# Overflow loop of an expert layer moved ahead of the last expert pair; last gathers made plain, their sums made on VectorE

## The chip, the cores and the metric

One core of one Trainium2 chip runs the program. The metric is the device time of one execution in microseconds. Before the change it is 790.01 us, the median of 3 runs (789.26 to 790.51).

## What is computed

One layer of a streaming encoder block on 512 tokens of width 1024, in float32: an input projection, a windowed attention and a state-space branch mixed by gates, a LayerNorm (h1), then the part that matters here:

```
g      = argmax of the 4 group logits of a token; its weight is the softmax value
e1, e2 = the two best of the 8 experts in that group, weights by softmax times the group's
moe    = sum over e1, e2 of weight * (silu(h1 @ w_gate[e]) * (h1 @ w_up[e])) @ w_down[e]
ple    = sigmoid(h1 @ w_ple_gate + b) * (p @ w_ple)
out    = LayerNorm(2**0.25 * h1 + moe + ple; ln2_w, ln2_b)
```

There are 32 experts, with matrices of 1024 x 256 (gate, up) and 256 x 1024 (down). Every token goes to two of them.

## The kernel before

**The expert stage.** Each expert gets 64 rows (`CAP`). Experts are worked off in 16 pairs of 128 rows; pair `p` has parity `p % 2`, and each parity has six weight slots of 1 MB in `ring` (parity 0: slots 0 to 5, parity 1: slots 6 to 11). SyncE loads a pair's weights as soon as the pair two before it has used its slots. GpSimd fetches the rows of a pair from `h1_dram` by an indirect DMA. TensorE turns them (`rows_turned_in`), multiplies them with gate and up (`gate_up`, L1256), ScalarE makes the tanh (`hidden_tanh`), VectorE the product (`hidden`, L2184 to L2189), TensorE turns that (`act_t`, L1281), ScalarE copies it (`act_copy`), TensorE multiplies with down (`down`, L1271). ScalarE and VectorE copy one half each of the result out of PSUM (`out_copy`, `out_half`), and GpSimd stores the 128 rows to `y_dram`, at places given by `storeU` (L844). Between these stand the pieces of `ple` (`ple_half`, `ple_sum`, `ple_out`), which add to `base`, the array that starts as 2**0.25 * h1 and in the end is the output.

**The last pair.** The result of pair 15 (`LAST`) is not stored. VectorE writes a matrix `last_rows` with each token's weight at the row where its result lies (`rows_weighted`, L2194 to L2202), TensorE turns it (`rows_turned`, L1287) and ScalarE copies it back (`last_rowsT`). In the kernel before this stands inside pair 14: TensorE turns it between `act_t` and `down` of pair 14. At the end TensorE multiplies `last_rowsT` with the pair's result, once for each of the 4 tiles of 128 tokens (`combine`, L1294), and VectorE adds the product to `base` (`added`, L2208).

**The overflow loop.** Rows beyond 64 of an expert would be worked off in a loop of up to 8 turns (`MORE_PAIRS`), whose body is entered only if the count in `ctl` asks for it. Each engine reads the count and goes through the 8 turns. With these inputs no turn is entered: the trace holds loads for exactly 32 experts. In the kernel before the loop stands after `gate_up` and `hidden` of the last pair and before its `act_t`.

**The gathers.** When the store of pair 14 has landed, GpSimd fetches for each tile the two result rows of each token from `y_dram` (L854), with a DMA that adds to `base`: the first results of tiles 0 to 3, then the second, each of which waits until the first of its tile has landed (`y_gath[i]`). `added` of a tile waits for both.

**The end.** ScalarE makes the LayerNorm sums of tiles 0 and 1 (`tile_stats`, L1382 to L1386: a sum pass and a square pass over 1024 elements), VectorE those of tiles 2 and 3 (L1676). TensorE spreads the rows ln2_w and ln2_b over the partitions by products with a one-row operand (L1360). Then VectorE makes the roots (L1681 and on) and normalizes tiles 0 to 2 in six passes (L1685, L1686); ScalarE and GpSimd do tile 3; ScalarE issues the four output DMAs.

The order of work of each engine is written out by hand; an engine goes through its queue in that order and waits where a `wait_ge` stands.

## Time and profile before

| | us |
|---|---|
| median of 3 runs | 790.01 (789.26 to 790.51) |
| profiled execution, its own time | 789.76 |
| its span, first to last instruction | 787.0 |
| TensorE busy | 728.7 (93%) |
| VectorE / ScalarE / GpSimd busy | 418.4 / 204.1 / 184.0 |
| DMA, mean rate over the span | 220 GB/s |

Busy times are sums over the span; the page's slices of 19.7 us show TensorE at 90% or more almost everywhere until the last few. In the eleven slices from 512 to 728 us, where the expert weights stream in, the DMA engines are at 90% or more, at 410 to 421 GB/s. What the change touches lies in the last 62 us. The difference between the execution's time and its span, 2.8 us, lies outside the instructions. The granted clock of TensorE has two levels here, shown as 1.00 (2.4 GHz) and 0.50 (1.2 GHz).

### The profile page before, as it was taken

The numbers are of one execution on the slowest core, as the hardware profiler recorded it, in microseconds if no ns is written. First come the engines' busy times: TensorE is split into PE (matmuls) and PEld (weight loads), VectorE is DVE, ScalarE is ACT, GpSimd is POOL, SyncE is SP. The second block draws the span as 40 slices with busy tenths as digits, with TensorE's granted clock in tenths as the row PEclk, the third lists the DMA queues.
The fourth block names the chain that finished last, engine by engine and source line by source line (L and its number), as shares of the span: only waits on it lengthen the run. The fifth ranks groups of instructions, "written<-read, shape, count | busy, mean of one in ns | idle before, by whom it ended". The sixth has DMA issues, their size and how long they took to land.

```text
span 787.0 us, 9738 instructions
## 1 busy us (share of the span) xinstructions
PE 728.7 (93%) x3799; PEld 512.9 (65%) x3799; DVE 418.4 (53%) x737; ACT 204.1 (26%) x358; POOL 184.0 (23%) x129
## 2 busy tenths in 40 slices
PE   4999999999999999999999999999999989897672
PEld 2897789998887878847888888445544444343220
DVE  6598946776678888655266957412121112121226
ACT  4313324555322223242041151111211121111030
POOL 4934490000041222002242003311111111111242
PEclk9999999999999999999999999999999999999985
DMA  9798131321031122243233298699999999999492
GB/s 309 268 410 201 58 108 54 94 69 54 4 105 54 54 54 54 65 176 110 104 143 152 102 399 329 215 419 415 415 410 417 421 419 419 421 420 416 154 201 107
DMA packets 61816, 173.15 MB, mean 220 GB/s; under 512 B 16982, under 2 KB 39712, under 8 KB 47946
## 3 DMA queue, kind: packets, MB, share of 16 engines
q1 hardware_dynamic: 52324, 141.79, 47.9%
q0 software_dynamic: 8752, 28.59, 11.1%
q10 hardware_dynamic: 694, 2.14, 0.7%
q8 instruction: 31, 0.51, 0.3%
q14 instruction: 15, 0.12, 0.0%
HBM read 155.52 MB, written 24.67 MB: 229 GB/s over the span
## 4 chain that ended last, share of the span: by engine, by line
PE 76%; DMA 12%; DVE 6%; issue 2%; POOL 1%; ACT 1%; SPq 0%; DVEq 0%; POOLq 0%
PE psum L902 37%; PE psum L1256 11%; DMA ring<-in_w_exp_up_dram 6%; PE psum L1271 5%; PE psum L1174 5%; PE psum L1111 3%; DMA ring<-in_w_in_dram 3%; PE psum L1060 2%; PE psum L1080 1%; PE psum L1212 1%; PE psum L1010 1%; DMA arena<-y_rows,rowsU 1%; PE psum L1177 1%; DMA arena<-in_w_ple_gate_dram 1%; PE psum L979 1%
## 5 line engine op out<-in xcount | busy, mean ns | idle before, releaser
L902 PE MATMUL psum<-ring_r 128*128 128x512 f32 (+1 forms) x928 | 247.5, 350 | 3.3 <-DVE arena_r L1695 1.7
L902 PEld LDWEIGHTS psum<-ring_r 128*128 128x128 f32 x928 | 164.1, 192 | 28.3 <-issue 3.2
L902 PE MATMUL psum<-arena_r,ring_r 128*128 128x512 f32 (+1 forms) x416 | 141.4, 377 | 0.0
L751 POOL TENSOR_TENSOR ring_r<-ring,ring_r 128x2048 fp32r<-128x2048 f32 x16 | 73.9, 4621 | 204.5 <-ACT ring_r L1369 204.5
L1256 PE MATMUL psum<-ring,arena 128*64 128x512 f32 x512 | 112.9, 593 | 5.3 <-DMA ring<-in_w_exp_up_dram 5.3
L1369 ACT COPY arena<-psum 128x512 f32<-128x512 f32 (+4 forms) x104 | 57.4, 580 | 172.3 <-PE psum L1271 55.8
L1256 PEld LDWEIGHTS psum<-ring,arena 128*64 128x64 f32 x512 | 39.5, 137 | 76.0 <-issue 76.0
L902 PEld LDWEIGHTS psum<-arena_r,ring_r 128*128 128x128 f32 x416 | 79.6, 191 | 13.7 <-issue 0.5
L1271 PE MATMUL psum<-ring,arena 128*64 128x512 f32 x256 | 61.1, 620 | 9.0 <-issue 9.0
L1174 PE MATMUL psum<-arena 128*128 128x256 f32 x256 | 64.5, 398 | 2.3 <-DVE rowsU L2153 1.2
L2184 DVE SCALAR_TENSOR_TENSOR arena<-arena,psum 128x256 f32<-128x256 f32 x16 | 9.7, 609 | 104.0 <-ACT arena L1584 103.9
L1174 PEld LDWEIGHTS psum<-arena 128*128 128x128 f32 x256 | 48.0, 197 | 20.3 <-issue 14.6
L1369 ACT CAST ring_r<-ring 128x2048 fp32r<-128x2048 f32 (+1 forms) x26 | 45.8, 1768 | 23.4 <-DMA ring<-in_w_in_dram 13.2
L1271 PEld LDWEIGHTS psum<-ring,arena 128*64 128x64 f32 x256 | 19.2, 142 | 41.4 <-issue 41.4
L2215 DVE COPY arena<-psum 128x512 f32<-128x512 f32 x16 | 11.1, 692 | 60.2 <-PE psum L1271 60.2
L902 PE MATMUL psum<-ring_r,arena_r 128*128 128x256 f32 (+1 forms) x144 | 41.4, 295 | 0.0
L810 POOL DMA_INDIRECT arena<-h_rows,info x14 | 14.3, 1021 | 115.6 <-PE psum L1212 106.9
L844 POOL DMA_INDIRECT y_rows<-arena,storeU x15 | 15.0, 1003 | 83.7 <-DVE arena L2215 83.0
L1584 ACT ACTIVATE arena<-psum 128x256 f32<-128x256 f32 x16 | 6.1, 384 | 106.2 <-PE psum L1256 106.2
L1496 ACT ACTIVATE ring<-psum,arena 128x512 f32<-128x512 f32 x16 | 11.0, 688 | 65.0 <-PE psum L902 65.0
L1111 PE MATMUL psum<-arena,ring 128*128 128x512 f32 x64 | 27.6, 592 | 0.0
L902 PEld LDWEIGHTS psum<-ring_r,arena_r 128*128 128x128 f32 (+1 forms) x144 | 26.0, 181 | 2.1
(299 smaller groups left out, 974.8 us busy)
## 6 DMA issues: line engine op xcount, KB each, us to landing
ring<-in_w_exp_up_dram SPq DMA_DIRECT2D x32, 1024.0 KB, 15.3
ring<-in_w_exp_down_dram SPq DMA_DIRECT2D x32, 1024.0 KB, 13.9
ring<-in_w_exp_gate_dram SPq DMA_DIRECT2D x32, 1024.0 KB, 11.2
ring<-in_w_in_dram SPq DMA_DIRECT2D x18, 1024.0 KB, 5.4
y_rows<-arena POOLq DMA_DIRECT2D x12, 1024.0 KB, 17.0
ring<-in_w_out_ssd_dram SPq DMA_DIRECT2D x4, 1024.0 KB, 6.5
ring<-in_w_out_dram SPq DMA_DIRECT2D x4, 1024.0 KB, 5.1
arena<-in_w_ple_gate_dram SPq DMA_DIRECT2D x4, 1024.0 KB, 12.8
```

Source lines behind the costliest of these rows:

```text
L751: g.tensor_tensor(lo, ring[:, SLOT_OF[seq]], hi.bitcast(F32), ALU.subtract).then_inc(s_w_lo, 1)
L810: g.indirect_dma_start(out=xg.rearrange("p k n -> p (k n)"), out_offset=None, in_=h1_dram, in_offset=bass.IndirectOffsetOnAxis(ap=tokens, ...
L844: g.indirect_dma_start(out=y_dram, out_offset=bass.IndirectOffsetOnAxis(ap=storeU[:, p:p + 1], axis=0), in_=eout[:, p % 2, :], in_offset=N ...
L902: t = mm(o, a, b, start=(first and j == 0), stop=(last and j == 2))
L1060: t = mm(o[:, m * P:(m + 1) * P], dta[:, c, hh:hh + 1].broadcast_to([P, P]), upper, start=True, stop=True)
L1111: t = mm(o, ringN[:, s, j % 2, n * P:(n + 1) * P], yaT[:, j, :], start=(j == 0), stop=(j == 3))
L1174: mm(ple_bank(n)[:, 0:PS], h1T[:, i, k, :], pgw[s][:, k, :], start=(k == 0), stop=(k == KD - 1))
L1256: t = mm(psum[sides[half], parity, :], xgT[parity][:, k, sides[half]], ring[:, s:s + 2, k, :], start=(k == 0), stop=(k == KD - 1))
L1271: t = mm(psum[sides[half], 4 + b, :], eactT[:, parity, k, sides[half]], ringN[:, s, k, b * 512:(b + 1) * 512], start=(k == 0), stop=(k == 1))
L1369: return nc.scalar.copy(dst, src)
L1496: A(gact[:, n, b, :], bank(("g", g)), ACT.Tanh, scale=0.5, bias=b_gate[:, 8 * b + n:8 * b + n + 1]).then_inc(s_g_read, 1)
L2215: v.tensor_copy(eout[:, u % 2, 512:1024], psum[:, 5, :]).then_inc(signal, 1)
```

## The change

- **Place of the loop.** On every engine the overflow loop now stands after pair 14 and before `gate_up` of pair 15. On TensorE each turn gets two transposes outside of the guarded body (the `nop` goes), and one more transpose after the loop signals `s_last_aT`.
- **Place of `last_rows`.** VectorE makes it after its copy of pair 14's result, TensorE turns it after `gate_up` of pair 15.
- **Rows of ln2.** The four one-row products stand before and after `act_t` and after `down` of pair 15, no longer at the end.
- **Gathers.** They no longer add: the first results go to slots 0 to 3 of `ring` (`first_res`, `second_res`), so they wait for TensorE to be past the loop (`s_last_aT >= 1`) and no longer for `base`. VectorE adds them (`result_in`): the four first ones before the copy of the last down product, each second one after that copy, before its tile's product is added.
- **Sum.** The add of a tile's product also makes the tile's sum (`added_last`, `tensor_tensor_reduce`); ScalarE makes the squares of all four tiles without a sum pass (`squares_about_mean`). VectorE's `tile_stats` at the end goes.
- `s_base_ready` goes; its waits on VectorE become waits of the common chain. `combine` and `added` take their banks as arguments.

```diff
 MOE_FREED = [("pe_ys", KD) if slot in (4, 5, 6, 7) else ("pe_mix", 2 * NT) for slot in range(12)]
+MORE_BANKS = ((6, 7), (4, 5))
+LAST_BANKS = ((1, 3), (4, 5))
...
...
@@ -846,15 +850,16 @@
                     in_offset=None, bounds_check=ROWS - 1, oob_is_err=False).then_inc(y_st[p % 2], 16)
             for parity in range(2):
                 pool.wait_ge(y_st[parity], 16 * (PAIRS // 2 - parity))
-            pool.wait_ge(s_base_ready, 4 * NT)
-            for c in range(2):
+            pool.wait_ge(s_last_aT, 1)
+            for c, to in enumerate((first_res, second_res)):
                 for i in range(NT):
                     if c:
                         pool.wait_ge(y_gath[i], 16)
                     g.indirect_dma_start(
-                        out=base[:, i, :], out_offset=None, in_=y_dram,
+                        out=to[:, i, :], out_offset=None, in_=y_dram,
                         in_offset=bass.IndirectOffsetOnAxis(ap=rowsU[:, 2 * i + c:2 * i + c + 1], axis=0),
-                        bounds_check=ROWS - 1, oob_is_err=True, compute_op=ALU.add).then_inc(y_gath[i], 16)
+                        bounds_check=ROWS - 1, oob_is_err=True).then_inc(y_gath[i], 16)
...
-                    break
+                rows_turned_in(p + 1)
                 if p == 0:
                     freed(3, 4, 5)
                 act_t(p, p % 2, p, s_aT_mm)
                 for n, half in after_act:
                     ple_half(n, half)
-                if p == LAST - 1:
-                    pe.wait_ge(s_last_rows, 1)
-                    rows_turned(last_rows, s_last_rows)
                 down(p, q, p % 2, (s_aT_sb, p + 1), s_y_mm)
                 for n, half in after_down:
                     ple_half(n, half)
-            pe.wait_ge(s_last_rows, 3)
             pe.wait_ge(s_ctl_ready, 1)
+            pe.wait_ge(s_pp_read, 4 * NT)
             pairs = pe.value_load(ctl[0:1, EXTRA + 1:EXTRA + 2], min_val=0, max_val=MORE_PAIRS)
             with pe.Fori(0, MORE_PAIRS) as j:
...
+                tr(psum[:, 6, 0:P], ident, ident)
+                tr(psum[:, 6, P:2 * P], ident, ident)
+
+            tr(psum[:, 6, 0:P], ident, ident).then_inc(s_last_aT, 1)
+            gate_up(LAST // 2, LAST % 2, 2 * PAIRS, s_last_aT)
+            pe.wait_ge(s_last_rows, 1)
+            rows_turned(last_rows, s_last_rows)
+            pe.wait_ge(s_ln_in, 64)
+
+            def ln2_row(row, b, to):
+
+                return mm(psum[:, to, :], ones[0:1, :], row[0:1, 512 * b:512 * b + 512], start=True, stop=True)
+
+            ln2_row(w_ln2, 0, W_BANKS[0])
+            ln2_row(w_ln2, 1, W_BANKS[1])
             act_t(LAST, LAST % 2, LAST, s_last_aT)
-            down(LAST, LAST // 2, LAST % 2, (s_last_aT, 2), s_last_y)
+            ln2_row(b_ln2, 1, B_BANKS[1])
+            down(LAST, LAST // 2, LAST % 2, (s_last_aT, 7), s_last_y)
+            pe.wait_ge(s_last_rows, 3)
+            ln2_row(b_ln2, 0, B_BANKS[0]).then_inc(s_pe_ln2, 1)
             pe.wait_ge(s_last_y, 3)
             for i in range(NT):
                 if i >= 2:
                     pe.wait_ge(s_last_added, i - 1)
-                combine(last_rowsT, LAST % 2, i, s_last_mm)
-            pe.wait_ge(s_ln_in, 64)
-            for j, row in enumerate((w_ln2, b_ln2)):
-                for b in range(2):
-                    t = mm(psum[:, 2 * j + b, :], ones[0:1, :], row[0:1, 512 * b:512 * b + 512], start=True, stop=True)
-            t.then_inc(s_pe_ln2, 1)
+                combine(last_rowsT, LAST % 2, i, LAST_BANKS[i % 2], s_last_mm)
...
                 act.wait_ge(s_act_sums, sums_made[0])
+
+            def squares_about_mean(x, i, scratch):
+
+                total, minus_mean, squares = (sums[:, i, j:j + 1] for j in range(3))
+                A(mva[:, i, 0:1], total, ACT.Copy, scale=1.0 / D)
+                summed(A(minus_mean, total, ACT.Copy, scale=-1.0 / D))
+                summed(A(scratch, x, ACT.Square, bias=minus_mean, accum_out=squares))
+                A(mva[:, i, 1:2], squares, ACT.Copy, scale=1.0 / D).then_inc(s_act_stats, 1)
...
                     out_copy((s_y_mm, j + LAST + 1), 16 * (PAIRS // 2), 0, s_y_act)
                 act.nop()
-            act_copy((s_last_aT, 1), LAST % 2, s_last_aT)
+            hidden_tanh((s_last_aT, 2), LAST % 2, s_last_aT)
+            rows_turned(last_rowsT, (s_last_rows, 2), s_last_rows)
+            act_copy((s_last_aT, 6), LAST % 2, s_last_aT)
             out_copy((s_last_y, 1), 16 * (LAST // 2), LAST % 2, s_last_y)
-            for i in range(2):
+            for i in range(NT):
                 act.wait_ge(s_last_added, i + 1)
-                tile_stats(base[:, i, :], i, h1_words[:, i, :])
+                squares_about_mean(base[:, i, :], i, h1_words[:, i, :])
             scaled(base[:, NT - 1, :], 1)
...
+                v.tensor_tensor(x, x, from_pe, ALU.add).then_inc(signal, 1)
+
+            def added_last(i):
+
+                dve.wait_ge(s_last_mm, i + 1)
+                banks = LAST_BANKS[i % 2]
+                from_pe = psum[:, banks[0]:banks[1] + 1:banks[1] - banks[0], :]
+                x = base[:, i, :].rearrange("p (b n) -> p b n", b=2)
+                v.tensor_tensor_reduce(out=x, in0=x, in1=from_pe, scale=1.0, scalar=0.0, op0=ALU.add, op1=ALU.add,
+                                       accum_out=sums[:, i, 0:1]).then_inc(s_last_added, 1)
+
+            def result_in(to, i, n):
+
+                dve.wait_ge(y_gath[i], 16 * n)
+                link(v.tensor_tensor(base[:, i, :], base[:, i, :], to[:, i, :], ALU.add))
             def out_half(made, stores, u, signal):
...
-                if p == LAST:
-                    break
                 for n in ple_done(p, 0, 1):
                     ple_sum(n)
                     ple_out(n)
-                if p == LAST - 1:
-                    dve.wait_ge(s_pe_pl, 4 * NT)
-                    rows_weighted(last_rows, -2 * CAP * LAST, 0, s_last_rows)
-                    dve.wait_ge(s_last_rows, 1)
-                    v.tensor_scalar(rowf, rowf, -float(2 * CAP * PAIRS), None, ALU.add).then_inc(s_weighted, 1)
-                    v.tensor_copy(rv[11], rv[8]).then_inc(s_more_added, 1)
                 out_half((s_y_mm, p + 1), 16 * q, p % 2, s_y_dve)
                 for n in ple_done(p, 2):
                     ple_sum(n)
                     ple_out(n)
+
+            dve.wait_ge(s_pe_pl, 4 * NT)
+            rows_weighted(last_rows, -2 * CAP * LAST, 0, s_last_rows)
+            dve.wait_ge(s_last_rows, 1)
+            v.tensor_scalar(rowf, rowf, -float(2 * CAP * PAIRS), None, ALU.add).then_inc(s_weighted, 1)
+            v.tensor_copy(rv[11], rv[8]).then_inc(s_more_added, 1)
...
+                result_in(first_res, i, 1)
             out_half((s_last_y, 1), 16 * (LAST // 2), LAST % 2, s_last_y)
             for i in range(NT):
-                dve.wait_ge(y_gath[i], 32)
-                added(i, (s_last_mm, i + 1), s_last_added)
-                if i >= 2:
-                    dve.wait_ge(s_last_added, i + 1)
-                    tile_stats(base[:, i, :], i)
-            dve.wait_ge(s_act_stats, 2 + 2)
+                result_in(second_res, i, 2)
+                added_last(i)
+            dve.wait_ge(s_act_stats, 2 + NT)
             dve.wait_ge(s_pe_ln2, 1)
-            w2, b2 = (psum[:, 2 * j:2 * j + 2, :].rearrange("p b n -> p (b n)") for j in range(2))
-            tiles_normed(base, w2, b2, s_fin_ready)
+            w2, b2 = (psum[:, banks[0]:banks[1] + 1:banks[1] - banks[0], :] for banks in (W_BANKS, B_BANKS))
+            tiles_normed(base.rearrange("p i (b n) -> p i b n", b=2), w2, b2, s_fin_ready)
 # ---- launch: one core; inputs and outputs as the reference has them ----
```

How the order moves. TensorE, from `act_t` of pair 14 on, before (L1287 turns `last_rows`, L1271 is `down` of pair 14, L1256 `gate_up` of pair 15, L1323 the load of the count ahead of the loop):

```order
L1281 MATMUL psum<-arena 128x128 [waits aT_sb,eact_sb]
L1281 MATMUL psum<-arena 128x128
L1287 MATMUL psum<-arena 128x128 [waits last_rows]
L1287 MATMUL psum<-arena 128x128 x3
L1271 MATMUL psum<-ring,arena 64x512 [waits y_act,aT_sb,y_dve,slot_in5,slot_in2]
L1271 MATMUL psum<-ring,arena 64x512 x7
L1256 MATMUL psum<-ring,arena 64x512 [waits slot_in10,slot_in9,xgT_sb,slot_in7,slot_in6]
L1256 MATMUL psum<-ring,arena 64x512 x15
L1323 TENSOR_LOAD ctl [waits ctl_ready,last_rows]
L1323 ISA x2
```

Now, the same place up to the load of the count:

```order
L1289 MATMUL psum<-arena 128x128 [waits aT_sb,eact_sb]
L1289 MATMUL psum<-arena 128x128
L1276 MATMUL psum<-ring,arena 64x512 [waits y_act,aT_sb,y_dve,slot_in5,slot_in2]
L1276 MATMUL psum<-ring,arena 64x512 x7
L1324 TENSOR_LOAD ctl [waits pp_read,ctl_ready]
```

and from the end of a turn of the loop (L1349, L1350 are its two transposes) through `gate_up` of pair 15 (L1261), the turning of `last_rows` (L1295) and the first row of ln2_w (L1360):

```order
L1349 MATMUL psum<-arena 128x128
L1350 MATMUL psum<-arena 128x128
L1325 REGISTER_ALU
L1325 COMPARE_AND_BRANCH
L1352 MATMUL psum<-arena 128x128
L1261 MATMUL psum<-ring,arena 64x512 [waits slot_in10,slot_in9,xgT_sb,slot_in7,slot_in6]
L1261 MATMUL psum<-ring,arena 64x512 x15
L1295 MATMUL psum<-arena 128x128 [waits last_rows]
L1295 MATMUL psum<-arena 128x128 x3
L1360 MATMUL psum<-arena 128x512 [waits ln_in]
```

`down` of pair 14 no longer has the turning of `last_rows` ahead of it; `gate_up` of pair 15 now has the whole loop ahead of it.

VectorE, from its copy of the last down product on, before:

```order
L2215 COPY arena<-psum 128x512 [waits y_st1,last_y]
L2208 TENSOR_TENSOR arena<-arena,psum 128x1024 [waits last_mm,y_gath0]
L2208 TENSOR_TENSOR arena<-arena,psum 128x1024 [waits last_mm,y_gath1]
L2208 TENSOR_TENSOR arena<-arena,psum 128x1024 [waits last_mm,y_gath2]
L1676 BN_STATS arena<-arena 128x6 [waits last_added]
L1676 BN_STATS arena<-arena 128x6 [waits dve_step]
L1677 BN_AGGR arena<-arena 128x2 [waits dve_step]
L2208 TENSOR_TENSOR arena<-arena,psum 128x1024 [waits last_mm,y_gath3,dve_step]
L1676 BN_STATS arena<-arena 128x6 [waits last_added]
L1676 BN_STATS arena<-arena 128x6 [waits dve_step]
L1677 BN_AGGR arena<-arena 128x2 [waits dve_step]
```

Now, from the last pair's hidden product on (L2199 and L2201; L2248 adds gathered rows, L2254 is the copy, L2242 the add with the sum and the read of its accumulator):

```order
L2199 SCALAR_TENSOR_TENSOR arena<-arena,psum 128x128x2 [waits last_aT]
L2201 TENSOR_TENSOR arena<-arena,psum 128x128x2 [waits last_aT]
L2248 TENSOR_TENSOR arena<-arena,ring 128x1024 [waits y_gath0]
L2248 TENSOR_TENSOR arena<-arena,ring 128x1024 [waits y_gath1,dve_step]
L2248 TENSOR_TENSOR arena<-arena,ring 128x1024 [waits y_gath2,dve_step]
L2248 TENSOR_TENSOR arena<-arena,ring 128x1024 [waits y_gath3,dve_step]
L2254 COPY arena<-psum 128x512 [waits y_st1,last_y,dve_step]
L2248 TENSOR_TENSOR arena<-arena,ring 128x1024 [waits y_gath0]
L2242 ISA arena<-arena,psum 128x1024 [waits last_mm,dve_step]
L2242 ISA arena 128x1
L2248 TENSOR_TENSOR arena<-arena,ring 128x1024 [waits y_gath1]
L2242 ISA arena<-arena,psum 128x1024 [waits last_mm,dve_step]
```

Four adds now stand ahead of the copy, and between two tiles' products there is one add of gathered rows, where the statistics of tiles 2 and 3 were.

## Rows read from the trace of the kernel before

**Rows 1.** Chain of waits at the end: start us, us, what.

```profile
728.95 2.20 DVE arena L2198 x8
...
731.92 1.09 PE psum L1287 x4
...
739.39 3.27 DMA y_rows<-arena,storeU
...
751.02 9.49 DMA arena<-y_rows,rowsU
...
767.21 4.82 PE psum L1360 x8
```

**Rows 2.** Timeline, 706 to 738 us: start us, us, engine, line, operation [idle before].

```profile
709.61 3.65 PE L1271 MATMUL psum<-ring,arena 128*64 128x512 f32 x16 [0.94 <-issue]
...
727.61 0.37 ACT L1369 COPY arena<-psum 128x256 f32<-128x256 f32 x1
...
737.85 0.69 DVE L2215 COPY arena<-psum 128x512 f32<-128x512 f32 x1 [5.70 <-PE psum L1271]
```

**Rows 3.** Timeline, 735 to 788 us.

```profile
737.63 7.03 PE L1256 MATMUL psum<-ring,arena 128*64 128x512 f32 x32
...
745.76 0.60 DVE L2189 TENSOR_TENSOR arena<-arena,psum 128x256 f32<-128x256 f32 x1
...
747.64 0.41 PE L1281 MATMUL psum<-arena 128*128 128x128 f32 x2 [2.98 <-issue]
...
749.60 5.05 PE L1271 MATMUL psum<-ring,arena 128*64 128x512 f32 x16 [1.55 <-issue]
...
760.54 1.22 DVE L2208 TENSOR_TENSOR arena<-arena,psum 128x1024 f32<-128x1024 f32 x1 [5.16 <-DMA arena<-y_rows,rowsU]
...
762.98 0.20 ACT L1383 ACTIVATE arena<-arena 128x1 f32<-128x1 f32 x1
...
764.58 0.20 ACT L1386 ACTIVATE arena<-arena 128x1 f32<-128x1 f32 x1
...
772.17 0.17 DVE L1681 TENSOR_SCALAR arena<-arena 128x4 f32<-128x4 f32 x1 [0.78 <-PE psum L1360]
...
781.02 1.28 DVE L1686 SCALAR_TENSOR_TENSOR arena<-arena,psum 128x1024 f32<-128x1024 f32 x1
```

**Rows 4.** Source view, PE's queue, L1323: ns min/median/max, first and last start us.

```profile
L1323 PEldq TENSOR_LOAD <-ctl x1: 489/489/489, 740.3 to 740.3; - x1
```

**Rows 5.** Source view, PE's loop (L1324): moves and end of turn.

```profile
L1324 PEldq MOVE  x9: 29/29/35, 741.2 to 746.8; - x9
...
L1324 PEldq COMPARE_BRANCH  x8: 86/224/240, 742.0 to 747.4; - x8
```

**Rows 6.** Source view, PE's queue at the waits of down and gate_up.

```profile
L1266 PEldq EVENT_SEMAPHORE  x2: 51/51/51, 732.0 to 749.5; - x2
```

**Rows 7.** Source view, the same at the next gate_up (L611).

```profile
L611 PEldq EVENT_SEMAPHORE  x1: 51/51/51, 733.5 to 733.5; - x1
```

**Rows 8.** Lines by form, DVE: busy us, mean ns.

```profile
L1937 DVE CUSTOM_DVE_ANT_0 arena<-arena 128x512 f32<-128x512 f32 x8 | 5.5, 692 | 0.3
...
L1898 DVE TENSOR_TENSOR arena<-arena 128x1024 f32<-128x1024 f32 x4 | 4.9, 1224 | 0.1
...
L1937 DVE DVE_READ_ACCUMULATOR2_ANT arena<- 128x1 f32 x8 | 0.7, 82 | 0.0
```

**Rows 9.** Lines by form, POOL.

```profile
L810 POOL DMA_INDIRECT arena<-h_rows,info x14 | 14.3, 1021 | 115.6 <-PE psum L1212 106.9 <-DMA info<-row_info 8.7
L854 POOL DMA_INDIRECT arena<-y_rows,rowsU x8 | 12.6, 1576 | 7.3 <-DMA arena<-y_rows,rowsU 3.1 <-DMA y_rows<-arena,storeU 3.0 <-issue 1.2
```

**Rows 10.** Source view of the gathers (L854), with their landing times.

```profile
L854 POOL DMA_INDIRECT arena<-y_rows,rowsU x8: 1559/1562/1661, 743.4 to 758.8; - x8
...
DMA to landing us min/median/max: 8.2/9.0/9.2
```

**Rows 11.** DMA issues around 726.6 us: us to landing.

```profile
arena<-in_ln_b_dram POOLq DMA_DIRECT2D x1, 512.0 KB, 10.9
```

**Rows 12.** DMA issues around 707.1 us.

```profile
ring<-in_w_exp_up_dram SPq DMA_DIRECT2D x1, 1024.0 KB, 26.5
```

**Rows 13.** Windows, PE alone: us, PE busy, granted clock, DMA share, GB/s.

```profile
745.60:749.04 3.44, 0.41 (x2) 1.00 0.98 155
749.05:752.45 3.40, 2.85 (x8) 0.50 1.05 184
752.50:762.69 10.19, 6.72 (x20) 1.00 1.06 209
```

78 lines of the change are left out of this document (39 added, 39 removed).

## The prediction

> **What bounds the kernel now.** I read the chain of waits first, backward from its end, then the timeline of the last 80 us, then the queue instructions, which the timeline leaves out. The reader is to see three stretches.
>
> *Ahead of `down` of pair 14.* ScalarE's copy of the turned activations ends at 727.98 [rows 2], so `down` could start at about 728.1. It starts at 733.01: VectorE first builds `last_rows` (L2198 from 728.95, 2.20 us) and TensorE turns it (731.92, 1.09 us) [rows 1]. It then runs until 737.82, and VectorE's copy starts at 737.85 [rows 2].
>
> *The gathers.* The store of pair 14 starts at 739.39 and takes 3.27 us [rows 1]. The eight gathers start between 743.4 and 758.8, about one per 2.2 us, each landing 8.2 to 9.2 us after its start [rows 10]. Tile 0's second one lands at 760.5 [rows 1]; VectorE sat idle 5.16 us before its first add at 760.54 [rows 3]. `down` of pair 15 had ended at 754.65 (749.60 and 5.05 us [rows 3]). So here the gathers bound the end, not the experts.
>
> *The end.* Adds, statistics and the one-row products (4.82 us, L1360 [rows 1]) run until the roots begin at 772.17; from there to the end of the last normalizing pass at 782.30 and of the span at 787.0 is 14.83 us [rows 3]. No step of that piece changes but for addresses; I count it at nothing.
>
> **The queue of TensorE** is the fourth thing to see. Its count is loaded at 740.3 [rows 4], and the eight turns run from 741.2 to about 747.6 (last branch 747.4) [rows 5], while the array still works on `gate_up` until 744.66 [rows 3]. The loop was thus mostly hidden; only 1.28 us show, since the hidden product was done at 746.36 and `act_t` began at 747.64 [rows 3]. The queue can run ahead: it went from the wait of `down` (732.0) to that of the next `gate_up` (733.5) in 1.5 us [rows 6, 7], while the array needed until 737.8.
>
> **Part by part.**
>
> *`last_rows` out of the way of `down` of pair 14.* `down` starts at 728.2. The same product for pair 13 took 3.65 us [rows 2], here it took 4.81 because it met the half clock. I take 3.65: it ends at 731.85, 5.97 us earlier. VectorE's copy (0.69) ends at 732.6, and `last_rows` follows: 2.20, 1.09 and small ones, done near 736, long before TensorE asks for it. It then costs nothing; without that cover it would cost the 3.2 us it took before.
>
> *The loop ahead of `gate_up` of pair 15.* The queue has issued `down` at 728.1 + 1.5 = 729.6. The load and the first turn begin 0.9 us apart (740.3, 741.2), so turns start at 730.7. A turn took 6.3/8 = 0.79 us [rows 5]. Now it issues two transposes, four records; the 32 records of `down` took 1.5 us to issue [rows 6, 7], 0.047 each, so 0.19 more: 0.98 a turn, 7.8 us, to 738.5. The transpose behind it and the waits of `gate_up` add 0.4: `gate_up` starts at **738.9**, 1.3 us later than the 737.63 of before, though the array is free from 731.85 on. Its weights are there: the last ones were issued at 707.0 and landed 26.5 us later, at 733.5 [rows 12]. So almost all of the 6 us are eaten by the loop. Bounds for a turn: 0.79 (transposes free, 1.5 us less in all) and 1.7 (each record of a transpose as dear as a branch, 0.224 [rows 5]; 5.8 us more). I take the rate at which `down` was issued, the nearest row.
>
> *`gate_up` to `down` of pair 15.* `gate_up` 7.03 us [rows 3], to 745.9. Behind it on TensorE now stand four transposes (0.44 at full clock) and two products of ln2_w. `gate_up` had 16 pairs of records in 7.03 us, 0.44 per pair; a full product is two records one after the other, so two products 1.7 us. They end at 748.1. The hidden product takes 1.70 us after `gate_up` (744.66 to 746.36 [rows 3]), to 747.6: `act_t` is now late by 0.5 because of the products ahead of it. It ends at 748.45, ScalarE's copy (0.37 [rows 2]) at 748.9, the product of ln2_b behind `act_t` ends at 749.3: `down` starts at **749.3**, 0.3 earlier than before. VectorE and ScalarE had done their loops by then.
>
> *The clock.* Before, `down` of pair 15 ran 3.4 us at 0.50 [rows 13], which cost it 5.05 - 3.65 = 1.4 us. In the new order the array is again lightly used ahead of it (transposes, one-row products), so I keep 5.05: `down` ends at 754.35, the copies at 755.1. Bounds: 1.4 less, or one more stretch at 0.50 in `gate_up`, 1.7 more (3.4 us do half the work).
>
> *Gathers.* The store is issued at 732.6 + 0.85 = 733.45, while weights and ln2_b still come in (the latter lands at 726.75 + 10.9 = 737.7 [rows 11], ahead of it in the same queue). I put its landing at 739.5. TensorE's signal comes at 738.6, so the first gather starts at 740.3, 3.1 us earlier. Plain row fetches take GpSimd 1.02 us, adding ones 1.58 [rows 9]. No unloaded plain fetch is in the trace; the nearest are the store (3.27) and the adding gathers (up to 9.2). I take about 4: the first results land from 744 to 749, the second ones until 754. VectorE's four first adds (1.224 each for two operands in SBUF [rows 8], 5.0 in all) start at 747.6 and are done at 752.6, hidden by `down`.
>
> *The adds at the end.* VectorE adds tile 0's second result by 756.3. TensorE makes the last ln2_b product (0.86) and tile 0's `combine` (1.7) from 754.35: 757.0. Each add with a sum: 512 elements took 692 ns, as a plain one of that size, plus an accumulator read of 82 [rows 8]; for 1024 I take 1.22 + 0.08 + gaps = 1.34, then the next tile's gathered add 1.25. Four tiles: 757.05 + 3 x 2.6 + 1.34 = 766.2. `combine` of tiles 1 to 3 (1.7, at half clock 3.4) keeps ahead. ScalarE's rest for the last tile took 762.98 to 764.78, 1.8 us [rows 3]: 768.05. The roots begin at **768.1** in place of 772.17: **4.1 us** earlier. The one-row products and VectorE's statistics are off the path.
>
> **Sum.** 789.76 - 4.1 = 785.7 for the profiled execution, which stands 0.25 below the median; in terms of the median 785.9. I say **785.8**. The 6 us that `down` of pair 14 gains are nearly all taken by the loop, so the last product is only 0.3 us earlier; the gain comes from the gathers, which no longer hold the first add (757.05 for 760.54). From that add to the roots it is 11.0 us, where it was 11.6. What is late next is VectorE.
>
> **Rivals.**
>
> 1. *The clock falls in the loop.* For: before, `act_t`'s two transposes were all that ran from 745.60 to 749.04 and the next 3.4 us were at 0.50 [rows 13]. Against: now 16 transposes run, some 0.22 of each 0.98 us. If `gate_up` meets 3.4 us of 0.50, the end is 1.7 later: 787.5; if `down` then meets none, 786.1. I say 787. The Trainium skill, TensorE: Matmul & The Clock Gate (Part 4, PE-mode transpose), holds that transposes do not count as array work for the clock; by it the loop's transposes are vain and this rival is the likelier. The trace agrees as far as the two transposes go, but it cannot tell them from idleness.
>
> 2. *The gathers still bound.* If plain ones move no faster than the adding ones, landings come 2.45 us apart from 749.3 on; the last of eight is in at 766.5, and 2.6 + 1.8 us later the roots begin at 770.9: 788.6. Against: adding ones read and write the same bytes, and the weight stream moved twice their 209 GB/s [rows 13] (410 to 421 by the page's slices).
>
> 3. *Slower: the loop's turns are dearer.* Place: TensorE's queue, with an empty array behind it. Each turn ends in a taken branch into code that now begins with array instructions. At the upper bound of 1.7 us a turn the loop ends at 744.3, `gate_up` starts 5.8 later than I forecast: 791.6. It decides from 1.5 us a turn on (4.1 us more, no gain). Against: all branches but the first took 0.22 with the queue full.
>
> 4. *Cheaper than forecast*: turns of 0.79 and no half clock ahead of `down`: 1.5 + 1.4 less, 782.9; with only one of the two 784.4.
>
> **Chances.** Forecast 0.47, rival 1 0.22, rival 2 0.08, rival 3 0.09, rival 4 0.14. A measurement can tell about 0.2% (1.6 us) from no change. Rival 3 gives slower 0.07, the rest no change; rival 2 is half no change; a bad end of rival 1 (half clock also in `combine`, 1.7 more) gives the rest of no change. Faster 0.82, same 0.11, slower 0.07. The range runs from 783.3 (part of rival 4) to 788.8 (all of rivals 1 and 2).
>
> **What would show it.** Right: `down` of pair 14 starts at about 728.2 and takes 3.7; the count is loaded near 729.8 and `gate_up` of pair 15 starts within 738 to 740 with nothing to wait for but its own queue; `down` of pair 15 starts near 749; VectorE never waits for a gather behind its last copy; its eight last adds are back to back but for the first; the roots begin near 768. Wrong: `gate_up` at 742 or later (rival 3); a clock of 0.50 under `gate_up` (rival 1); VectorE waiting for `y_rows` (rival 2); an add with a sum that takes over 1.5 us; or a change ahead of 726 us, which no step here foresees.

## The result, and the profile after

The changed kernel takes **784.05 us** (median of 7 runs, 783.24 to 786.09), beside 790.01 us for the kernel before (7 runs on the same chip, 787.93 to 790.96): ratio 0.9931, 95% interval 0.9915 to 0.9946. It is faster by 5.4 us by that ratio (4.3 to 6.7). The forecast was 785.8, with 783.3 to 788.8 as its range. Run again on another chip (`changed_again` below), the kernel gave 0.9918 (0.9894 to 0.9942).

| | before | after |
|---|---|---|
| median, us | 790.01 | 784.05 |
| profiled execution, its own time | 789.76 | 785.12 |
| its span | 787.0 | 783.4 |
| TensorE busy | 728.7 | 727.8 |
| VectorE busy | 418.4 | 425.3 |

The two profiled executions show 3.6 us of span, less than the medians do. One reason is upstream: in the profile of after, ScalarE's copy ahead of `down` of pair 14 ends at 728.88, 0.9 us later than before (727.98 [rows 2]), though nothing ahead of it was changed. So I count from that copy's end, called the anchor here. From it to the roots before took 772.17 - 727.98 = 44.19 us [rows 2, 3]; after it takes 768.51 - 728.88 = **39.63 us**, 4.6 less. From the roots to the end of the span it is 14.9 us, as before (14.8).

The chain of waits of the changed kernel ends like this (start us, us, what):

```profile
729.09 3.67 PE psum L1276 x16
734.38 7.66 DMA y_rows<-arena,storeU
746.83 6.13 DMA ring<-y_rows,rowsU
755.07 5.41 PE psum L1301 x8
```

The building of `last_rows` and the one-row products of [rows 1] are gone from it. The store and a gather are still in it, and the store's piece has grown from 3.27 to 7.66 us.

The timeline of the changed kernel, 728 to 747 us (L1276 is `down`, L1349 the transposes of the loop, L1261 `gate_up`, L848 the store, L858 the gathers, L1289 `act_t`):

```profile
728.51 0.37 ACT L1381 COPY arena<-psum 128x256 f32<-128x256 f32 x1
729.09 3.65 PE L1276 MATMUL psum<-ring,arena 128*64 128x512 f32 x16 [1.24 <-issue]
...
732.84 0.69 DVE L2254 COPY arena<-psum 128x512 f32<-128x512 f32 x1 [3.23 <-PE psum L1276]
...
734.38 1.02 POOL L848 DMA_INDIRECT y_rows<-arena,storeU  x1 [6.18 <-DVE arena L2254]
...
736.49 0.33 PE L1349 MATMUL psum<-arena 128*128 128x128 f32 x1 [0.40 <-issue]
...
737.00 7.09 PE L1261 MATMUL psum<-ring,arena 128*64 128x512 f32 x32
742.83 1.08 POOL L858 DMA_INDIRECT ring<-y_rows,rowsU  x1 [7.42 <-DMA y_rows<-arena,storeU]
...
746.52 0.44 PE L1289 MATMUL psum<-arena 128*128 128x128 f32 x2
```

`down` of pair 14 starts 0.2 us behind the anchor and takes 3.65 us, where it had started 5.0 us behind it and taken 4.81. `gate_up` starts right behind the loop's last transpose and waits for no weights. GpSimd stands idle 7.42 us on the store.

The source views of the changed kernel's count load (L1324) and of its turns (L1325), ns min/median/max, first and last start:

```profile
L1324 PEldq TENSOR_LOAD <-ctl x1: 487/487/487, 729.3 to 729.3; - x1
...
L1325 PEldq COMPARE_BRANCH  x8: 86/224/247, 731.1 to 736.6; - x8
```

The load comes 0.2 us behind the start of `down`, and seven turns take 736.6 - 731.1 = 5.5 us, 0.79 each; before they took 747.4 - 742.0 = 5.4 [rows 5].

The timeline from 747 us on (L2248 adds gathered rows, L2254 is the copy of the last down product, L1301 `combine`, L2242 the add with the sum, L1698 the roots):

```profile
747.57 1.23 DVE L2248 TENSOR_TENSOR arena<-arena,ring 128x1024 f32<-128x1024 f32 x1 [1.78 <-DMA ring<-y_rows,rowsU]
747.94 3.65 PE L1276 MATMUL psum<-ring,arena 128*64 128x512 f32 x16
...
749.61 1.23 DVE L2248 TENSOR_TENSOR arena<-arena,ring 128x1024 f32<-128x1024 f32 x1 [0.81 <-DMA ring<-y_rows,rowsU]
...
751.32 1.23 DVE L2248 TENSOR_TENSOR arena<-arena,ring 128x1024 f32<-128x1024 f32 x1 [0.49 <-DMA ring<-y_rows,rowsU]
...
753.06 1.23 DVE L2248 TENSOR_TENSOR arena<-arena,ring 128x1024 f32<-128x1024 f32 x1 [0.51 <-DMA ring<-y_rows,rowsU]
...
754.32 0.69 DVE L2254 COPY arena<-psum 128x512 f32<-128x512 f32 x1
754.93 1.22 DVE L2248 TENSOR_TENSOR arena<-arena,ring 128x1024 f32<-128x1024 f32 x1
755.07 8.83 PE L1301 MATMUL psum<-arena 128*128 128x512 f32 x16 [2.42 <-DVE arena L2254]
757.68 1.22 DVE L2242 CUSTOM_DVE_ANT_1 arena<-arena,psum 128x1024 f32<-128x1024 f32 x1 [1.53 <-PE psum L1301]
...
760.61 1.22 DVE L2242 CUSTOM_DVE_ANT_0 arena<-arena,psum 128x1024 f32<-128x1024 f32 x1 [0.57 <-PE psum L1301]
...
765.41 1.22 DVE L2242 CUSTOM_DVE_ANT_0 arena<-arena,psum 128x1024 f32<-128x1024 f32 x1
...
768.51 0.17 DVE L1698 TENSOR_SCALAR arena<-arena 128x4 f32<-128x4 f32 x1 [1.87 <-ACT arena L1397]
```

Here is what bounds it now. `down` of pair 15 ends at 751.59, but VectorE copies its product only at 754.32: it waited for each of the four first results and stands in their adds. 2.7 us of the last pair's earliness are lost there.

The source views of the changed kernel's gathers (L858) with their landing times:

```profile
L858 POOL DMA_INDIRECT ring<-y_rows,rowsU x8: 1003/1225/1437, 742.8 to 753.7; - x8
...
DMA to landing us min/median/max: 4.7/5.6/6.1
```

They land in 5.6 us (median), where the adding ones took 9.0 [rows 10], and start 1.6 us apart on average.

Windows of the changed kernel, TensorE alone (us, busy, granted clock, DMA share, GB/s), under `gate_up`, `down` of pair 15 and a part of `combine`:

```profile
737.00:744.10 7.10, 7.10 (x34) 1.00 0.13 51
...
747.90:751.60 3.70, 3.70 (x18) 1.00 0.91 293
...
756.50:759.80 3.30, 3.30 (x5) 0.50 0.47 181
```

The half clock (1.2 GHz), which lay on `down` of pair 15 before [rows 13], now lies on `combine`, where it shows as VectorE's two waits for L1301.

### The profile page after: what moved, and what is told of

It reads as the page before. It is cut to its first block, busy times and chain, and to the rows that moved or that the text cites. A ratio compares the mean times of both kernels' runs of the same rounds, so it can differ in the third digit from the quotient of the medians.

```text
span 783.4 us, 9786 instructions
## 1 busy us (share of the span) xinstructions
PE 727.8 (93%) x3816; PEld 512.6 (65%) x3816; DVE 425.3 (54%) x743; ACT 205.1 (26%) x364; POOL 181.0 (23%) x129
## 4 chain that ended last, share of the span: by engine, by line
PE 76%; DMA 12%; DVE 6%; issue 2%; ACT 1%; POOL 1%; SPq 0%; DVEq 0%; POOLq 0%
PE psum L907 37%; PE psum L1261 12%; DMA ring<-in_w_exp_up_dram 6%; PE psum L1179 5%; PE psum L1276 5%; PE psum L1116 4%; DMA ring<-in_w_in_dram 3%; PE psum L1065 2%; PE psum L1085 2%; PE psum L1217 1%; PE psum L1015 1%; PE psum L1182 1%; DMA arena<-in_w_ple_gate_dram 1%; PE psum L984 1%; DMA y_rows<-arena,storeU 1%
## 5 line engine op out<-in xcount | busy, mean ns | idle before, releaser
L1261 PE MATMUL psum<-ring,arena 128*64 128x512 f32 x512 | 114.6, 600 | 3.7 <-DMA ring<-in_w_exp_up_dram 3.7
L1261 PEld LDWEIGHTS psum<-ring,arena 128*64 128x64 f32 x512 | 40.1, 138 | 74.7 <-issue 74.6
L1276 PE MATMUL psum<-ring,arena 128*64 128x512 f32 x256 | 58.5, 598 | 8.7 <-issue 8.7
L1179 PEld LDWEIGHTS psum<-arena 128*128 128x128 f32 x256 | 48.5, 198 | 20.7 <-issue 14.8
L1276 PEld LDWEIGHTS psum<-ring,arena 128*64 128x64 f32 x256 | 18.6, 136 | 39.5 <-issue 39.5
L2254 DVE COPY arena<-psum 128x512 f32<-128x512 f32 x16 | 11.1, 692 | 49.4 <-PE psum L1276 49.4
L848 POOL DMA_INDIRECT y_rows<-arena,storeU x15 | 15.1, 1003 | 77.5 <-DVE arena L2254 77.2
```

The lines of the kernel that those rows point to most:

```text
L848: g.indirect_dma_start(out=y_dram, out_offset=bass.IndirectOffsetOnAxis(ap=storeU[:, p:p + 1], axis=0), in_=eout[:, p % 2, :], in_offset=N ...
L1179: mm(ple_bank(n)[:, 0:PS], h1T[:, i, k, :], pgw[s][:, k, :], start=(k == 0), stop=(k == KD - 1))
L1261: t = mm(psum[sides[half], parity, :], xgT[parity][:, k, sides[half]], ring[:, s:s + 2, k, :], start=(k == 0), stop=(k == KD - 1))
L1276: t = mm(psum[sides[half], 4 + b, :], eactT[:, parity, k, sides[half]], ringN[:, s, k, b * 512:(b + 1) * 512], start=(k == 0), stop=(k == 1))
L2254: v.tensor_copy(eout[:, u % 2, 512:1024], psum[:, 5, :]).then_inc(signal, 1)
```

## The experiments

Two theories. **G**: the store, the gathers and VectorE's first adds ahead of the copy bound the end of the changed kernel. **L**: the last pair on TensorE does, with the loop ahead of it. "Roots at" and "copy at" give the start of the roots and of VectorE's copy of the last down product, counted from the anchor; they come from one profiled execution each. A ratio is to runs of the kernel before on the same chip. Not all runs were made on one chip, so I compare ratios where I can.

| run | median us (runs) | ratio to before | copy at | roots at |
|---|---|---|---|---|
| before | 790.01 (7) | | 26.71 | 44.19 |
| the change | 784.05 (7) | 0.9931 (0.9915 to 0.9946) | 25.44 | 39.63 |
| `changed_again` | 783.45 (6) | 0.9918 (0.9894 to 0.9942) | 24.55 | 37.74 |
| `one_turn` | 783.83 (4) | 0.9926 (0.9910 to 0.9943) | 24.89 | 38.08 |
| `no_loop_transposes` | 785.66 (4) | 0.9953 (0.9937 to 0.9970) | 25.65 | 38.98 |
| `last_rows_back` | 787.22 (7) | 0.9969 (0.9956 to 0.9982) | 29.03 | 42.73 |
| `adding_gathers` | 787.40 (10) | 0.9966 (0.9955 to 0.9978) | 25.90 | 42.21 |
| `copy_after_two` | 783.78 (6) | 0.9936 (0.9911 to 0.9961) | 22.70 | 37.38 |
| `copy_first` | 786.19 (10) | 0.9958 (0.9940 to 0.9976) | 22.58 | 40.09 |
| `ln_rows_after_store` | 783.28 (6) | 0.9925 (0.9900 to 0.9949) | 22.71 | 36.03 |
| `sum_pass_back` | 786.70 (10) | 0.9978 (0.9960 to 0.9995) | 25.15 | 40.88 |
| `late_rows_new_order` | 781.88 (6) | 0.9890 (0.9867 to 0.9912) | 23.57 | 35.96 |
| `guarded_loop` | 783.21 (6) | 0.9906 (0.9880 to 0.9932) | 25.72 | 39.80 |

**`changed_again`**, no edit. It tells how far two profiles of one kernel lie apart.

> The changed kernel once more, on the chip of the next two runs, so that they have it beside them. Both theories expect what it gave before: about 784 us, ratio to the kernel before 0.991 to 0.995, 39.6 us from the end of ScalarE's copy ahead of down of pair 14 to the roots.

Its time is as expected, its roots come at 37.74, not 39.6: **1.9 us between two profiles of the same kernel**. Its window on `combine`, and its first add with a sum:

```profile
753.00:757.00 4.00, 3.98 (x10) 1.00 0.70 260
```

```profile
755.16 1.22 DVE L2242 CUSTOM_DVE_ANT_1 arena<-arena,psum 128x1024 f32<-128x1024 f32 x1 [1.07 <-PE psum L1301]
```

There is no half clock under `combine`, so the first add waits 1.07 us and not 1.53, and the second follows without a wait (1.0 us of the 1.9 in all); its store landed in 7.1 us, and VectorE's copy came 0.9 us earlier. A difference of less than some 2 us between the last column's numbers says nothing by itself; I use the rows that say what waited, and the ratios. Part of this spread goes with the clock: of the 13 runs of the changed kernel, the six with a mean granted clock of 0.984 or more took 782.01 to 784.05 us, the six with 0.981 or less 783.71 to 786.09. A profile shows only one of them.

**`one_turn`**: the loop on TensorE has one turn (the seven others, which matter only where rows overflow, are left out).

```diff
-            with pe.Fori(0, MORE_PAIRS) as j:
+            with pe.Fori(0, 1) as j:
```

> TensorE's overflow loop goes one turn in place of eight (the other seven would only matter with overflow, which these inputs don't have). Theory G: in the changed kernel the end is set by the gathers: VectorE's copy of the last down product stands behind four adds that wait for them, 2.7 us after down of pair 15 has ended (751.59, copy at 754.32), and the gathers wait for the store of pair 14 (landed 742.04), not for the loop (over at 736.7). So seven turns less (5.4 us) move gate_up and down of pair 15 forward by 3 us or more (gate_up then waits for its weights) and the end by less than 0.5 us: 784.0, 783.4 to 784.6. Rival L: the loop is on the path; the end comes 3 us earlier: about 781.

`gate_up` and the copy (timeline), and a window under the first part of `gate_up` with all engines (after the span: PE, PEld, DVE, ACT, POOL, then clock, DMA share, GB/s):

```profile
735.50 8.78 PE L1261 MATMUL psum<-ring,arena 128*64 128x512 f32 x32 [2.14 <-DMA ring<-in_w_exp_up_dram]
...
753.90 0.69 DVE L2254 COPY arena<-psum 128x512 f32<-128x512 f32 x1
```

```profile
735.50:738.80 3.30, 3.30 (x10) 1.21 (x12) 1.40 (x5) 0.00 (x0) 0.05 (x1) 0.54 0.50 200
```

`gate_up` starts 6.49 us behind the anchor (729.01 here) instead of 8.12, now held by its weights, and runs 8.78 us instead of 7.09, its first 3.3 us at a granted clock of 0.54. It ends 15.27 us behind the anchor, in the change 15.21. The time is the same. So a shorter loop alone bought nothing here, since the clock took back what it gave. This run does not show what an earlier `down` of pair 15 would be worth.

**`no_loop_transposes`**: the loop's turn ends in a `nop` again.

```diff
-                tr(psum[:, 6, 0:P], ident, ident)
-                tr(psum[:, 6, P:2 * P], ident, ident)
+                pe.nop()
```

> The two transposes of each turn go, a nop stands there as in the kernel before. Clock: if they hold the granted clock, gate_up of pair 15 now meets 3.4 us of 0.50 and lasts 8.7 us in place of 7.1; if they do nothing for it, gate_up stays at 7.1. A turn should stay at 0.77 us less 0.02 to 0.2. Theory G: a later down of pair 15 is hidden up to 2.7 us, so the time stays within 0.5 us of 784.05 either way; Rival L: 1.6 us later if the clock falls, 785.7.

Windows under `gate_up` and `down` of pair 15:

```profile
735.54:738.90 3.36, 3.00 (x7) 0.50 0.35 139
...
749.20:752.50 3.30, 3.30 (x10) 0.50 0.92 331
```

In the two profiles of the change the clock was 1.00 in both places. For `gate_up` this is shown: it takes 8.39 us without the transposes, and 7.09 in each of the nine profiles here that have all eight turns with them. For `down` it is not. It takes 5.35 us here, but two kernels that keep the transposes meet the half clock there too: `last_rows_back` (5.35 us) and `adding_gathers`, whose TensorE program is that of the change:

```profile
747.82 5.99 PE L1276 MATMUL psum<-ring,arena 128*64 128x512 f32 x16
```

In the other seven of the nine, `down` takes 3.65 us.

Without the transposes a turn is 0.77 us long (branches at 730.4 to 735.8), with them 0.79 in most profiles: they cost some 0.02 us a turn. `gate_up` starts 7.97 us behind the anchor without them and 7.94 to 8.17 with them (`last_rows_back`, where all is later, left out). The Trainium skill, TensorE: Matmul & The Clock Gate (Part 4, PE-mode transpose), says that the full clock doesn't engage for transposes and that they don't count as array work in the same way. Here the granted clock under `gate_up` says that they count, for they are all that differs. What that is worth in time stays unclear: by the ratios 1.7 us, but the intervals overlap, and the profile shows the cost mostly hidden by the gathers (copy at 25.65, held by `down` for 1.40 us).

**`last_rows_back`**: `last_rows` is built and turned ahead of `down` of pair 14 again.

```diff
+                if p == LAST - 1:
+                    pe.wait_ge(s_last_rows, 1)
+                    rows_turned(last_rows, s_last_rows)
                 down(p, q, p % 2, (s_aT_sb, p + 1), s_y_mm)
```

(with the same move on ScalarE and VectorE)

> last_rows is made and turned inside pair 14 again, ahead of its down product, as in the kernel before. down of pair 14 then starts 4.9 us later (and may meet the half clock, 1.2 more), the store is issued 5 to 6 us later. Theory G: the store then lands faster, because weights and ln2 rows are in by then (3.3 us as before, not 7.7), so it lands only 1.0 to 2.0 us later, the gathers start that much later and so does the end: 785 to 786.5. Rival L (the last pair bounds): the loop and all behind it move by 5 to 6 us, less the slack of 2.7: 786.5 to 787.5. If the whole 5 to 6 us come back, 789.5.

```profile
751.47 5.35 PE L1276 MATMUL psum<-ring,arena 128*64 128x512 f32 x16
...
756.92 0.69 DVE L2257 COPY arena<-psum 128x512 f32<-128x512 f32 x1 [2.18 <-PE psum L1276]
```

By the ratios the move is worth 0.9969 - 0.9931 = 0.0038, 3.0 us; the two intervals together leave some 1.6 us either way. But L's account holds here, not G's: the gathers start only 1.3 us later (their store, with the loads ahead of it landed before it starts, lands in 3.3 us), and the copy waits for `down`, not for a gather. `down` of pair 15 starts 4.5 us later than in the change (23.58 us behind the anchor for 19.06) and ends 6.2 later, since it meets the half clock as well (5.35 us for 3.65). The two chains lie about 2.7 us apart, so the copy comes 3.6 us later and the last pair is the bound. Some of the 3.0 us is thus the clock's, not the move's.

**`adding_gathers`**: the gathers add to `base` again, VectorE's adds of gathered rows go.

```diff
-                        out=to[:, i, :], out_offset=None, in_=y_dram,
+                        out=base[:, i, :], out_offset=None, in_=y_dram,
...
-                        bounds_check=ROWS - 1, oob_is_err=True).then_inc(y_gath[i], 16)
+                        bounds_check=ROWS - 1, oob_is_err=True, compute_op=ALU.add).then_inc(y_gath[i], 16)
```

> The gathers add to base in the DMA again; VectorE's eight adds of gathered rows go. Theory G: adding gathers land 2.45 us apart, from a first start at 742.8: first results by 759, the second ones of tiles 0 to 3 at about 760, 762.4, 765, 767.3; the last add with its sum then ends at 768.7, 2.1 us later than 766.6: 786.2 (785.5 to 787). If VectorE's adds were what bounds (rival), taking eight of them away would gain: 782 or less.

```profile
759.81 1.22 DVE L2242 CUSTOM_DVE_ANT_1 arena<-arena,psum 128x1024 f32<-128x1024 f32 x1 [5.25 <-DMA arena<-y_rows,rowsU]
...
767.08 1.22 DVE L2242 CUSTOM_DVE_ANT_0 arena<-arena,psum 128x1024 f32<-128x1024 f32 x1 [1.29 <-DMA arena<-y_rows,rowsU]
```

Every last add waits for a gather, 5.25 us the first, the last ones 2.45 us apart; each lands in 9.5 us (median). That `down` met the half clock here did not set the time: it ended at 753.81, and VectorE then still waited for a gather until 759.81. Plain gathers are worth 2.8 us by the ratios (0.9966 - 0.9931 = 0.0035 of 790, some 1.5 us either way).

**`copy_after_two` and `copy_first`**: VectorE's copy stands behind two of the first results, or ahead of all.

```diff
-            for i in range(NT):
+            for i in range(2):
                 result_in(first_res, i, 1)
             out_half((s_last_y, 1), 16 * (LAST // 2), LAST % 2, s_last_y)
+            for i in range(2, NT):
+                result_in(first_res, i, 1)
```

> VectorE copies the last down product after the first results of tiles 0 and 1, and adds those of tiles 2 and 3 after it. Theory G (in the changed kernel the copy stands 2.7 us behind its product because the adds ahead of it wait for gathers): the copy comes at 751.7 in place of 754.3, combine of tile 0 and 1 is done before VectorE asks for it (no waits of 1.5 and 0.6), and the roots begin 1.5 to 2.2 us earlier: 782.2 (781.5 to 782.8). If VectorE's sum of work after the copy is what counts (rival), two more adds behind the copy (2.5 us) cancel it: 784.

> The copy of the last down product stands ahead of all first results. Theory G: the copy comes at 751.7, but VectorE idles until then (the gathers of tiles 0 and 1 landed at 747.6 and 749.6), and all eight gathered adds follow: the last add with its sum ends at 751.7 + 0.7 + 8 x 1.23 + 4 x 1.17 = 766.9, about as now (766.6): 784.3 (783.6 to 785). If holding the copy were the whole loss (rival), it would gain the 2.7 us: 781.5.

`copy_after_two`:

```profile
751.28 0.69 DVE L2254 COPY arena<-psum 128x512 f32<-128x512 f32 x1 [0.95 <-PE psum L1276]
751.89 3.73 DVE L2248 TENSOR_TENSOR arena<-arena,ring 128x1024 f32<-128x1024 f32 x3
```

`copy_first`:

```profile
752.21 0.69 DVE L2254 COPY arena<-psum 128x512 f32<-128x512 f32 x1 [5.85 <-PE psum L1276]
752.82 6.25 DVE L2248 TENSOR_TENSOR arena<-arena,ring 128x1024 f32<-128x1024 f32 x5
```

Both bring the copy up to the end of `down`. With `copy_first` the 5 us of first adds then all stand behind it and the first add with a sum comes later than in the change: nothing gained (2.1 us lost by the ratios, just beyond the two intervals taken together). With `copy_after_two` two of them do, and the roots come 2.3 us earlier than in the first profile of the change, 0.4 than in the second; its ratio is that of the change. So the wait of the copy is real, and moving the copy alone is not worth what can be measured: VectorE has twelve adds of 1.2 us to do, and each one that no longer stands ahead of the copy stands behind it (eight in the change, ten with `copy_after_two`, twelve with `copy_first`).

**`ln_rows_after_store`**: the loads of ln2_w and ln2_b stand behind the store of pair 14 in GpSimd's queue.

```diff
-                if p == LAST - 1:
-                    pool.wait_ge(s_pe_pl, 4 * NT)
-                    for dst, name in ((w_ln2, "ln2_w"), (b_ln2, "ln2_b")):
-                        pool.dma_start(dst, aps[name].broadcast_to([P, D])).then_inc(s_ln_in, 16)
...
+            pool.wait_ge(s_pe_pl, 4 * NT)
+            for dst, name in ((w_ln2, "ln2_w"), (b_ln2, "ln2_b")):
+                pool.dma_start(dst, aps[name].broadcast_to([P, D])).then_inc(s_ln_in, 16)
```

> GpSimd issues the loads of ln2_w and ln2_b (512 KB each) after the store of pair 14, no longer before it. The store took 7.7 us from start to landing in the changed kernel, 3.3 in the one before, where it came 5 us later. Theory Q (it queues behind the ln2 loads): it lands 2 to 3 us sooner, the gathers start 1.5 to 3 us sooner, the copy is then held by down of pair 15 only: 782.3 (781.5 to 783.3). Theory W (it shares the DMA engines with the weights of pair 15): it still takes 7 us and more, 784; and if the ln2 loads now delay the first gathers, up to 785.5.

Source view of the store (L844), the copy, and for the change the issue of the second load:

```profile
DMA to landing us min/median/max: 3.3/3.3/3.3
```

```profile
751.77 0.69 DVE L2253 COPY arena<-psum 128x512 f32<-128x512 f32 x1 [1.06 <-PE psum L1275]
```

```profile
arena<-in_ln_b_dram POOLq DMA_DIRECT2D x1, 512.0 KB, 11.9
```

The store lands in 3.3 us instead of 7.7, the gathers start 9.57 us behind the anchor instead of 13.95, and now the copy waits for `down`. G's wait ahead of the copy is gone. Theory W, the sharing with the weights, does not carry the delay either: in the change the DMA engines are busy for 0.26 of the time from 738 to 739 us (mean of the 16) and for 0.12, 0.09 and 0.02 in the next three, and yet the store lands at 742.04. Which of the engines still had work then, these views do not show. The Trainium skill, DMA: Bandwidth & Descriptors (Queues, rings and completion order), says that each DMA engine takes turns between its queues. By its section Two DMAs through the same engine are not ordered, descriptors within one queue of an engine start in order. The trace agrees: in the change the store stood behind the two loads in one queue and landed 2.5 us after the second of them (issued at 727.64, landed 11.9 us later), and taking them out of its way brought it back to 3.3. In the next two kernels, which have the same order, it took 4.5 and 5.0 us, so the loads ahead are the larger part of the delay but perhaps not all of it. Roots at 36.03 are 1.7 and 3.6 us ahead of the two profiles of the change; by the runs (783.28, 781.07 to 785.88) the gain is not shown.

**`sum_pass_back`**: the last add is a plain one, ScalarE makes a sum pass and a square pass again.

```diff
-                squares_about_mean(base[:, i, :], i, h1_words[:, i, :])
+                tile_stats(base[:, i, :], i, h1_words[:, i, :])
...
-                v.tensor_tensor_reduce(out=x, in0=x, in1=from_pe, scale=1.0, scalar=0.0, op0=ALU.add, op1=ALU.add,
-                                       accum_out=sums[:, i, 0:1]).then_inc(s_last_added, 1)
+                v.tensor_tensor(x, x, from_pe, ALU.add).then_inc(s_last_added, 1)
```

> VectorE's add of the product makes no sum; ScalarE makes it in a pass of its own for all four tiles. ScalarE then needs 2.9 to 3.0 us a tile where VectorE needs 2.4, so it falls behind: its last tile ends at 758.9 + 4 x 2.95 = 770.7 in place of 768.5: 786.2 (785.3 to 787). If only the last tile's extra pass counts, 1.25 us: 785.3.

```profile
769.97 0.17 DVE L1698 TENSOR_SCALAR arena<-arena 128x4 f32<-128x4 f32 x1 [4.50 <-ACT arena L1406]
```

VectorE waits 4.50 us behind its last add where it waited 1.87: 2.6 us for the sum, and the add itself costs the same 1.22. By the ratios it is 0.9978 - 0.9931 = 0.0047, 3.7 us (some 1.8 us either way), which agrees.

**`late_rows_new_order` and `guarded_loop`**: the late loads, and on VectorE the second result of tile 0 ahead of the copy; then the same with the loop inside a question and 24 transposes in place of its turns.

```diff
+            result_in(second_res, 0, 2)
             out_half((s_last_y, 1), 16 * (LAST // 2), LAST % 2, s_last_y)
-            for i in range(NT):
+            result_in(second_res, 1, 2)
+            added_last(0)
+            added_last(1)
+            for i in range(2, NT):
```

```diff
-            with pe.Fori(0, MORE_PAIRS) as j:
-                with pe.If(pairs > j):
+            with pe.If(pairs > 0):
+                with pe.Fori(0, MORE_PAIRS) as j:
+                    with pe.If(pairs > j):
...
+            for _ in range(24):
```

> Both gains of the earlier runs in one kernel: the loads of ln2_w and ln2_b behind the store of pair 14 (so that it lands in about 3.3 us), and on VectorE first results, second result of tile 0, copy, second result of tile 1, then the adds with sums. Theory G (gathers and the order of VectorE set the end, until down of pair 15 does): the copy comes 22.7 us after the anchor (end of ScalarE's copy ahead of down of pair 14), held by down of pair 15, and the roots at 34 to 35 us (36.03 with the late loads alone, 37.38 with copy_after_two alone), about 781.5 us. If the two gains are one and the same (both only make VectorE's copy earlier), it gives no more than ln_rows_after_store alone: roots at 36.0, about 783.

> late_rows_new_order, and each engine's loop stands inside a question whether the count is above 0, so that its 8 turns cost one branch; 24 transposes stand where the turns were, to keep the array busy until the weights are in. Gate_up then starts with the last weights, about 6.5 us after the anchor in place of 8.1. If down of pair 15 bounds by now (theory G with the gathers out of the way): everything behind is 1 to 1.5 us earlier, roots at 32.5 to 33.5, about 780. If the gathers still bound, it is the same as late_rows_new_order. If the clock falls under gate_up in spite of the transposes, gate_up takes 8.4 to 8.8 us and nothing is gained either; the granted clock under it tells this case from the last.

Roots at 35.96 against 36.03, as the second case had it. But this does not show that the two gains are one and the same: in this profile the store took 4.5 us to land, not 3.3, the gathers started 1.2 us later than in `ln_rows_after_store`, and the add put ahead of the copy, which waited for its row, holds it 0.8 us past the end of `down`. The kernel has the lowest median of all, 781.88. The change on the same chip had 783.45, and five of the six runs here lie below all six of it (its lowest is 782.01), so a gain over the change is likely, though the two intervals against the kernel before overlap.

`guarded_loop`, windows under `gate_up` and `down` of pair 15, and from the timeline the latter's row, the add ahead of VectorE's copy, and the copy:

```profile
733.90:741.00 7.10, 7.10 (x34) 1.00 0.73 217
744.70:748.10 3.40, 3.40 (x9) 0.50 0.92 336
```

```profile
745.17 6.65 PE L1276 MATMUL psum<-ring,arena 128*64 128x512 f32 x16
...
751.68 1.23 DVE L2251 TENSOR_TENSOR arena<-arena,ring 128x1024 f32<-128x1024 f32 x1 [1.41 <-DMA ring<-y_rows,rowsU]
...
752.94 0.69 DVE L2257 COPY arena<-psum 128x512 f32<-128x512 f32 x1
```

`gate_up` starts at 6.67 as expected, at full clock, and ends 1.5 us earlier. Then `down` meets the half clock for nearly its whole length and takes 6.65 us in place of 3.65: it ends 24.6 us behind the anchor, in `late_rows_new_order` 22.8. None of the three expected cases foresaw this one: the clock held in `gate_up` and fell one product later. The gathers still bound as well: the second result of tile 0 kept VectorE waiting 1.41 us, and so the copy came 1.1 us after the end even of this late `down`. What a last pair that is earlier and at full clock would be worth is therefore open.

## Why the prediction was right

It is faster, as forecast, and the time lies in the range. The sum from anchor to roots was right to half a microsecond for the first profile: 768.1 - 727.98 = 40.1 us forecast, 39.63 measured. (The second profile, at 37.74, is off by 2.4.) That closeness is luck: inside the sum large terms were wrong and cancelled, and the case that the forecast describes did not come out as it stands. The median, 784.05, is nearest to what rival 4 gives with one of its two terms, 784.4.

- *`down` of pair 14 at once, in 3.65 us*: right to the hundredth. `last_rows` later costs nothing: right; undone, it cost 3.0 us, in part through the clock.
- *The loop eats almost all of it; `gate_up` at 738.9*: **wrong by 2.8 us**. It started 8.12 us behind the anchor, not 10.9. Two terms failed. The queue's 1.5 us to issue `down`, read between two waits of the queue [rows 6, 7], was no issuing time: the count load came 0.2 us behind `down`'s start. What filled the 1.5 us before was not tried. And 0.047 us per record gave 0.19 us for a turn's two transposes, which cost some 0.02. Both bounds of the turn were given; the near one held.
- *The clock, 5.05 us for `down` of pair 15*: **wrong, 3.65** in both profiles of the change. The forecast took an array with nothing but transposes and one-row products for lightly used; `no_loop_transposes` shows that they keep the clock up under `gate_up`. That they keep it up under `down` is not shown: `adding_gathers`, with the same TensorE program, took 5.99. In the first profile of the change the half clock came later, under `combine`, and cost 1.0 us; in the second there was none. Rival 1 did not happen.
- *The store lands at 739.5, 6.05 us after its issue*: **7.66**. The loads ahead of it were seen but priced too low: with them out of its way the gathers started 4.4 us earlier. The landing at 739.5 was an estimate with no row behind it.
- *Plain gathers land in about 4 us, so that VectorE's first adds are hidden by `down`*: **wrong**, and this is the step that hid the others. They took 4.7 to 6.1 and started 1.3 to 2.0 us apart. VectorE waited for every first result, and its copy came 2.7 us after `down` of pair 15. The sign I named for rival 2 ("VectorE waiting for `y_rows`") was there, not behind the copy but ahead of it, and at 1.7 to 2.0 us a gather and not 2.45.
- *2.6 us per tile at the end*: 2.4, and ScalarE's rest 1.9 for 1.8. The forecast had priced the sum in the add only through these 1.8 us and did not say what it saves; undone, the wait grew by 2.6 us.

So `down` of pair 15 ended 3.7 us earlier than forecast (751.59 against 754.35 + 0.9 for the later anchor), and the copy, held by the gathers, only 1.0 us. Rival 4 named what happened to TensorE (short turns, no half clock in `down`) and gave 782.9; the median did not reach it, since the second chain, the gathers, lay just behind the first. The parts, each undone alone, are worth 3.0, 2.8 and 3.7 us by the ratios, more together than the 5.4 us of the change: I read this as each one taken back leaving a bound that the others no longer help. No run puts the loop back behind `gate_up`, or the rows of ln2 back to the end, so what these two moves are worth by themselves is open.
